# Attention by pairs of heads: two heads side by side in the TensorE array, values as the standing operand, probabilities scaled ahead of their transposes

## The chip, the cores and the metric

The kernel runs on one core of a Trainium2 chip, as one program written by hand for five engines: TensorE (PE in the profile, PEld for its weight loads), VectorE (DVE), ScalarE (ACT), GpSimd (POOL) and SyncE (SP), which issues the transfers. The metric is device time in microseconds (us), the median of several runs.

## The reference, cut to what matters

A block of two transformer layers and a second block of one layer, for 256 tokens of width 1024, all in float32. Each of the three layers has an attention, and these are what the change touches:

```python
# layer 0: 8 heads of 128 + 64 rotary; a query of chunk c (64 tokens) sees the keys of chunks <= c
s = (einsum('bqhd,bkhd->bhqk', qn, k_nope) + einsum('bqhr,bkr->bhqk', qr, k_rope)) * scale
p = softmax(where(key_chunk <= q_chunk, s, -inf));  o = einsum('bhqk,bkhd->bqhd', p, v);  y = o @ w_o
...
# layer 1: 16 heads of 64, a bias by relative position
p = softmax(where(valid, einsum('bnqhd,bnkhd->bnhqk', q, k_band) * 64**-0.5 + bias, -inf))
o = einsum('bnhqk,bnkhd->bnqhd', p, v_band) @ w_o
...
# second block: 8 heads of 64 by softmax with a bias, and 8 heads of 64 by stick-breaking
z = einsum('bhqd,bhkd->bhqk', qb, k) * scale
log_keep = where(past, log_sigmoid(-z), 0)
a = where(past, exp(log_sigmoid(z) + cumsum_from_the_right(log_keep) - log_keep), 0)
ob = einsum('bhqk,bhkd->bhqd', a, v)
```

With 256 tokens there are two blocks of 128 queries. Queries of the first block see only the first 128 keys, those of the second all 256, so the scores of a head are 128 x 128 and 128 x 256, stored as 128 partitions (queries) by 384 columns.

## The kernel before, in words

Activations stand transposed (features on partitions, 256 tokens along the columns). Every weight product is done in three float32r matmuls (high weight by high x, high by low, low by high: lines 448 to 450), and such a triple on one 128 x 128 weight tile is called a unit here. Weights come in pieces of 16 units (1 MB); ACT rounds a piece to its high half (L785, `whi`), DVE subtracts to get the low half (L1163, `wlo`), into three buffers each, so both run up to three pieces ahead of PE and wait for PE to finish a piece. Attention matmuls are plain float32, and each of these stands in the trace as two matmul records (two passes over the array).

An attention never stands alone on PE: the function `_mixed` deals its steps out between the units of the two weight products around it, and all engines walk the same list. Stage 0 is layer 0 (units of `wuq`, the query projection, then of `wo0`, the output projection), stage 1 is layer 1 (`wq1`, `wo1`), stage 2 the second block (`win_q`, then `win_g`, with eight softmax heads and then eight stick heads). For each head h:

- `scores` (L536, L538): PE multiplies queries by keys into a PSUM bank. Heads of 64 use 64 of the array's 128 rows; in stage 0 a full product is followed by two rotary parts on 32 rows. DVE adds the mask or bias and takes the row maximum (`biased`, L1217 and L1219), makes the exponent's offset (`least`, L1225), and ACT takes the exponential with its row sum (`exps`, L825 and L826).
- `turn` (L547): three transposes of the 128 x 384 probabilities; ACT copies them out of PSUM (`turned`, L834, tile `PT`).
- `values` (L557 to L559): the transposed probabilities are the standing operand and the head's values stream through, which gives queries on partitions; DVE scales by the inverse row sum while it copies to tile `O` (`output`, L1244).
- `chunk` (L567, L568): two transposes bring `O` (one head of 128 or two of 64) back to features on partitions; ACT makes the high half (`oh`, L839) and DVE the low half (`ol`, L1252) that the output projection reads.

Stick heads have `sticks` (L719, L720) for `scores`, then ACT, DVE and POOL work and `sums` (L725 to L727, sums of logarithms by a triangular matrix) before `values`. Four PSUM banks go round for the attention. An output projection's unit k*8 may not start before `chunk` k is done. The queries of a head must first be taken out of PSUM (`scaled_out`, L1261, on DVE), which stands in DVE's list at the last unit of their pair of tiles.

Of the kernel before, what the change touches and what calls it, by code (L numbers as in the profile page):

```python
# [7 lines left out]
F32 = mybir.dt.float32  # L8
# [84 lines left out]
def _soft_steps(heads, depth, per):  # L93

    ahead, whole = [], []
    for h in list(heads) + [None] * depth:
        before = ahead.pop(0) if len(ahead) == depth or (h is None and ahead) else None
        if before is not None:
            yield "turn", before
        if whole:  # L100
            yield "chunk", whole.pop(0)
        if h is not None:
            yield "scores", h
            ahead.append(h)
        if before is not None:
            yield "values", before
            if before % per == per - 1:
                whole.append(before // per)
    yield "chunk", whole.pop(0)


def _stick_steps(heads):
    ahead, whole = [], []
    for h in list(heads) + [None] * 2:
        before = ahead.pop(0) if len(ahead) == 2 or (h is None and ahead) else None
        if before is not None:
            yield "sums", before
        if whole:
            yield "chunk", whole.pop(0)
        if h is not None:  # L120
            yield "sticks", h
            ahead.append(h)
        if before is not None:
            yield "values", before
            if before % 2 == 1:
                whole.append(before // 2)
    yield "chunk", whole.pop(0)


def _mixed(units, steps, paces, head_at, chunk_name):  # L130
# [7 lines left out]

    for unit in units:
        if unit[0] == chunk_name:  # L140
            while unit[1] // 8 not in made:
                made.add(peek()[1] if peek()[0] == "chunk" else None)
                yield ahead.pop(0)
        yield unit
        done.add(unit)
        credit += paces[unit[0]]
        while credit >= 1:
            credit -= 1
            step = peek()
            if step is None or (step[0] in ("scores", "sticks") and head_at(step[1]) not in done):  # L150
                continue
            if step[0] == "chunk":
                made.add(step[1])
            yield ahead.pop(0)
# [1667 lines left out]
```

## Time and profile before

| | |
|---|---|
| three runs, median (lowest to highest) | 1096.03 us (1093.57 to 1100.73) |
| the profiled execution, its own time | 1088.3 us |
| its span, first to last instruction | 1086.6 us |
| mean granted TensorE clock | 0.974 |
| PE busy, PEld busy | 94%, 90% of the span |
| DVE busy, ACT busy | 67%, 50% |
| HBM read | 191.93 MB, 178 GB/s over the span |

Busy time of PE is made of modelled, overlapping records, so a matmul's cost is better read from the start of one record to the start of the next than from its length. The profile's span is 1.7 us below its execution's own time, and that is 0.7% below the median of the three runs.

### The profile page before, as it was taken

How to read it: one execution, taken by the hardware profiler on the slowest of the kernel's cores; microseconds unless marked ns; L12 is line 12 of the kernel's file. 1: busy time of each engine (PE TensorE's matmuls, PEld its weight loads, DVE VectorE, ACT ScalarE, POOL GpSimd, SP SyncE). 2: the span in 40 equal slices, each digit the busy share in tenths (PEclk: the TensorE clock that was granted, in tenths of full speed). 3: DMA queues.
4: the chain of work that ended last, by engine and by line, in shares of the span. 5: the costliest groups of instructions: out<-in, count | busy, mean ns of one | idle time of the engine just before them, and what ended most of it. 6: DMA issues, size and time to landing. Idle time of an engine off the chain costs nothing.

```text
span 1086.6 us, 19070 instructions
## 1 busy us (share of the span) xinstructions
PE 1022.5 (94%) x8068; PEld 976.2 (90%) x8068; DVE 729.1 (67%) x1300; ACT 538.4 (50%) x818; POOL 31.3 (3%) x50
## 2 busy tenths in 40 slices
PE   5989899999997999989999998899999989999997
PEld 5968799999996988879999996798999979999996
DVE  5845487787658855489786876545553776888762
ACT  6624464445434544455443432545664456666641
POOL 0000000000004000000000002000120000000000
PEclk9989999999998999999999998999999999999999
DMA  7512247666744723228665784352224344545541
GB/s 263 216 66 99 97 147 266 235 233 258 292 172 156 281 95 116 80 83 306 259 249 202 309 318 173 131 195 102 93 102 156 132 178 156 186 177 185 191 156 40
DMA packets 27877, 194.21 MB, mean 179 GB/s; under 512 B 3088, under 2 KB 3344, under 8 KB 4880
## 3 DMA queue, kind: packets, MB, share of 16 engines
q1 hardware_dynamic: 27792, 192.99, 48.5%
q8 instruction: 64, 1.05, 0.4%
q14 instruction: 21, 0.17, 0.0%
HBM read 191.93 MB, written 1.05 MB: 178 GB/s over the span
## 4 chain that ended last, share of the span: by engine, by line
PE 71%; DVE 13%; ACT 11%; issue 3%; DMA 1%; SPq 0%; POOL 0%; DVEq 0%; POOLq 0%; ACTq 0%
PE bank L448 19%; PE bank L450 18%; PE bank L449 18%; ACT s_whi L785 6%; DVE s_xT L1290 2%; PE bank L538 2%; DVE s_tmp L1613 2%; DVE s_tmp L1615 2%; PE bank L536 2%; PE bank L487 2%; DVE s_wlo L1163 2%; PE bank L489 1%; PE bank L488 1%; DVE s_tmp L1286 1%; ACT s_tmp L1123 1%
## 5 line engine op out<-in xcount | busy, mean ns | idle before, releaser
L1163 DVE TENSOR_TENSOR s_wlo<-s_raw,s_whi 128x512 fp32r<-128x512 f32 (+1 forms) x352 | 371.1, 1091 | 155.0 <-ACT s_whi L785 154.6
L448 PE MATMUL bank<-s_hh,s_whi 128*128 128x256 f32 x1560 | 447.3, 287 | 24.6 <-DVE s_wlo L1163 12.8
L449 PE MATMUL bank<-s_hl,s_whi 128*128 128x256 f32 x1560 | 438.4, 281 | 0.0
L450 PE MATMUL bank<-s_hh,s_wlo 128*128 128x256 f32 x1560 | 438.1, 281 | 0.0
L785 ACT ACTIVATE s_whi<-s_raw 128x1024 fp32r<-128x1024 f32 (+2 forms) x223 | 303.5, 1385 | 223.5 <-PE bank L450 209.2
L448 PEld LDWEIGHTS bank<-s_hh,s_whi 128*128 128x128 f32 x1560 | 298.9, 192 | 33.6 <-issue 15.4
L450 PEld LDWEIGHTS bank<-s_hh,s_wlo 128*128 128x128 f32 x1560 | 298.6, 191 | 0.0
L449 PEld LDWEIGHTS bank<-s_hl,s_whi 128*128 128x128 f32 x1560 | 298.2, 191 | 0.1
L448 PE MATMUL bank<-s_ph,s_whi 128*128 128x256 f32 x528 | 146.1, 277 | 0.5 <-DVE s_wlo L1163 0.5
L450 PE MATMUL bank<-s_ph,s_wlo 128*128 128x256 f32 x528 | 146.0, 277 | 0.0
L449 PE MATMUL bank<-s_pl,s_whi 128*128 128x256 f32 x528 | 146.0, 276 | 0.0
L448 PEld LDWEIGHTS bank<-s_ph,s_whi 128*128 128x128 f32 x528 | 99.1, 188 | 0.7 <-DVE s_wlo L1163 0.7
L450 PEld LDWEIGHTS bank<-s_ph,s_wlo 128*128 128x128 f32 x528 | 99.3, 188 | 0.0
L449 PEld LDWEIGHTS bank<-s_pl,s_whi 128*128 128x128 f32 x528 | 99.1, 188 | 0.0
L825 ACT ACTIVATE s_S<-s_S,s_small 128x128 f32<-128x128 f32 x32 | 12.8, 402 | 78.2 <-DVE s_small L1225 78.1
L1185 DVE SCALAR_TENSOR_TENSOR s_adacc<-s_raw,s_cact,s_adacc 128x2048 f32<-128x2048 f32 x21 | 49.2, 2344 | 0.0
L448 PE MATMUL bank<-s_oh,s_whi 128*128 128x256 f32 x128 | 38.0, 297 | 2.8 <-DVE s_Q L1261 1.7
L1406 DVE TENSOR_TENSOR s_tmp<-bank,s_R 128x256 f32<-128x256 f32 x44 | 18.5, 420 | 32.3 <-PE bank L450 32.3
L1613 DVE SCALAR_TENSOR_TENSOR s_tmp<-bank,s_cols,s_tmp 128x255 f32<-128x255 f32 (+1 forms) x44 | 21.2, 482 | 25.4 <-ACT s_tmp L1123 24.6
L487 PE MATMUL bank<-s_whi,s_hh 128*128 128x512 f32 x64 | 27.7, 433 | 8.6 <-DVE s_hl L1205 5.9
L449 PE MATMUL bank<-s_ol,s_whi 128*128 128x256 f32 x128 | 35.6, 278 | 0.0
L450 PE MATMUL bank<-s_oh,s_wlo 128*128 128x256 f32 x128 | 35.5, 278 | 0.0
(207 smaller groups left out, 1277.9 us busy)
## 6 DMA issues: line engine op xcount, KB each, us to landing
s_raw<-in_gu SPq DMA_DIRECT2D x44, 1024.0 KB, 4.9
s_raw<-in_dn SPq DMA_DIRECT2D x33, 1024.0 KB, 5.0
s_raw<-in_wada SPq DMA_DIRECT2D x24, 1024.0 KB, 5.4
s_raw<-in_up SPq DMA_DIRECT2D x22, 1024.0 KB, 4.9
s_raw<-in_wo SPq DMA_DIRECT2D x8, 1024.0 KB, 4.8
s_raw<-in_win_g SPq DMA_DIRECT2D x8, 1024.0 KB, 4.8
s_raw<-in_wkv_v SPq DMA_DIRECT2D x4, 1024.0 KB, 5.0
s_raw<-in_wkv_k SPq DMA_DIRECT2D x4, 1024.0 KB, 7.9
```

Of the source, the lines that this page charges most:

```text
L448: e.matmul(out, hi, xh[:, k, :], start=first, stop=False, skip_group_check=True)
L449: e.matmul(out, hi, xl[:, k, :], start=False, stop=False, skip_group_check=True)
L450: m = e.matmul(out, lo, xh[:, k, :], start=False, stop=last, skip_group_check=True)
L487: e.matmul(out, xh[:, k, xk], hi, start=k == 0, stop=False)
L536: e.matmul(bank[:, 0:P], x[:, 0:P], y[:, 0:P], start=i == 0, stop=i == n - 1)
L538: m = e.matmul(bank[:, P:384], x[:, P:T], y, start=i == 0, stop=i == n - 1)
L785: e.activation(whi[w % SPLIT][:, at], raw[p % RAW][:, at], ACT.Copy).then_inc(S.hi.tick((w, c0)), 1)
L1163: e.tensor_tensor(wlo[s][:, at], raw[p % RAW][:, at], whi[s][:, at].bitcast(F32), ALU.subtract).then_inc(S.lo.tick((i, j), (i, "all")), 1)
L1185: m = e.scalar_tensor_tensor(out=adacc[:, :], in0=src, scalar=cact[:, kc:kc + 1], in1=adacc[:, :], op0=ALU.mult, op1=ALU.add)
L1290: e.tensor_tensor(xT[:, j, :], xT[:, j, :], u[:, :], ALU.add).then_inc(S.resid.tick((nxt, j), (name, j)), 1)
L1613: e.scalar_tensor_tensor(out=v[:, shift:T], in0=bank[:, 0:T - shift], scalar=col(name, n), in1=v[:, shift:T], op0=ALU.mult, op1=ALU.add)
L1615: m = e.scalar_tensor_tensor(out=g[:, shift:T], in0=bank[:, T:2 * T - shift], scalar=col(name, NF + n), in1=g[:, shift:T], op0=ALU.mult, o ...
```

## The change: what it does

The step of the list is now a pair of heads, and the list has new steps (`scale`, `exp`). Five things differ:

- `scores` and `sticks` write two heads into two banks, with the matmuls of the two heads in turn. The heads of a pair lie on different rows of the array (rows 0 to 63 and 64 to 127; in stage 0 the rotary parts on neighbouring groups of 32 rows).
- `scale` (`normal`): DVE multiplies the probabilities by the inverse row sum in SBUF, before the transposes, in four instructions a pair.
- `values`: the head's values stand in the array and the transposed probabilities stream, so the result comes with features on partitions. Heads of 64 go to output partitions 0 to 63 and 64 to 127 of one bank (two halves of the array's columns). `output`, the tile `O` and the PE step `chunk` are gone; ACT and DVE make `oh` and `ol` straight from the bank, in stage 0 for two heads (512 columns) at once.
- the list deals pairs out by other paces; `scale`, `exp` and `chunk` take no place of their own on PE.
- the buffers: two `S` of two heads for three of one; the second `PT` of stages 0 and 1 lies in tiles `adacc` and `yb`; in stage 2 five banks go round; POOL's and ACT's stick work is done by pairs, two of ACT's three functions in one instruction for both heads.

```diff
+def _soft_steps(pairs):
+    pairs = list(pairs)
+    for i in range(-2, len(pairs)):
+        now, nxt, new = ((pairs[j:j + 1] if j >= 0 else []) for j in (i, i + 1, i + 2))
+        for p in new:
+            yield "scores", p
+        for p in now:
+            yield "values", p
+        for p in nxt:
+            yield "scale", p
+        for p in new:
+            yield "exp", p
+        for p in now:
+            yield "chunk", p
+        for p in nxt:
+            yield "turn", (p, 0)
+            yield "turn", (p, 1)
...
-    return _mixed(_units("wuq") + _units("wo0"), _soft_steps(range(8), 1, 1), {"wuq": 0.4, "wo0": 0.5},
-                  lambda h: ("wuq", 12 + 6 * (h // 2) + 5), "wo0")
+    return _mixed(_units("wuq") + _units("wo0"), _soft_steps(range(4)), {"wuq": 0.3, "wo0": 0.3},
+                  lambda p: ("wuq", 12 + 6 * p + 5), "wo0", 2)
...
-    return _mixed(_units("wq1") + _units("wo1"), _soft_steps(range(16), 2, 2), {"wq1": 0.6, "wo1": 0.6},
+    return _mixed(_units("wq1") + _units("wo1"), _soft_steps(range(8)), {"wq1": 0.35, "wo1": 0.35},
...
-                for i, (x, y) in enumerate(parts):
-                    e.matmul(bank[:, 0:P], x[:, 0:P], y[:, 0:P], start=i == 0, stop=i == n - 1)
-                for i, (x, y) in enumerate(parts):
-                    m = e.matmul(bank[:, P:384], x[:, P:T], y, start=i == 0, stop=i == n - 1)
...
+                for i, heads in enumerate(parts):
+                    last = i == len(parts) - 1
+                    for blk, cols_, rows in ((0, slice(0, P), P), (1, slice(P, 384), T)):
+                        for a, (x, y) in enumerate(heads):
+                            m = e.matmul(pair_banks[a][:, cols_], x[:, blk * P:(blk + 1) * P], y[:, 0:rows],
+                                         start=i == 0 and blk == 0, stop=last, skip_group_check=True)
...
-                e.matmul(bank[:, 0:dv], p[:, 0:P], A.V[:, 0, v], start=True, stop=True)
-                e.matmul(bank[:, dv:2 * dv], p[:, P:T], A.V[:, 0, v], start=True, stop=False)
-                e.matmul(bank[:, dv:2 * dv], p[:, T:384], A.V[:, 1, v], start=False, stop=True).then_inc(
-                    S.attn.tick((s, "values", h)), 1)
-            def chunk(s, A, c, per, b=None):
...
-                e.transpose(bank[:, 0:P], A.O[c % 2][:, 0, :], ident[:, :])
-                e.transpose(bank[:, P:T], A.O[c % 2][:, 1, :], ident[:, :]).then_inc(S.attn.tick((s, "chunk", c)), 1)
+                for kb, keys in ((0, slice(0, T)), (1, slice(T, 384))):
+                    for a in range(2):
+                        v = A.V[:, kb, (2 * p + a) * dv:(2 * p + a + 1) * dv]
+                        if dv == P:
+                            out, first = bank[:, a * T + kb * P:(a + 1) * T], a == 0 and kb == 0
+                        else:
+                            out, first = bank[a * dv:(a + 1) * dv, kb * P:T], kb == 0
+                        m = e.matmul(out, v, probs[:, a, keys], start=first, stop=kb == 1, skip_group_check=True)
+                m.then_inc(S.attn.tick((s, "values", p)), 1)
...
+            def normal(s, A, p):
+                w = small[p % 3]
+                q.wait_ge(S.soft, (s, "exp", p))
+                e.reciprocal(w[:, 12:16], w[:, 8:12]).then_inc(S.score.tick((s, p, "inverse")), 1)
+                q.wait_ge(S.score, (s, p, "inverse"))
+                for a in range(2):
+                    sc = A.S[p % 2][:, a, :]
+                    for blk, at in ((0, slice(0, P)), (1, slice(P, 384))):
+                        i = 2 * a + blk
+                        m = e.tensor_scalar(sc[:, at], sc[:, at], w[:, 12 + i:13 + i], None, ALU.mult)
+                    m.then_inc(S.score.tick((s, p, "scaled", a)), 1)
...
-                elif step == "values":
-                    output("o0", A0, i, P)
+                elif step == "scale":
+                    normal("o0", A0, i)
```

**PE in stage 1.** Before, where one head's scores and another's values stand (`qh`, `ql`: the layer's input; `bank`: PSUM):

```order
L536 MATMUL bank<-s_K,s_Q 128x128
L538 MATMUL bank<-s_K,s_Q 128x256
L448 MATMUL bank<-s_qh,s_whi 128x256
L449 MATMUL bank<-s_ql,s_whi 128x256
L450 MATMUL bank<-s_qh,s_wlo 128x256
L557 MATMUL bank<-s_V,s_PT 128x64
L558 MATMUL bank<-s_V,s_PT 128x64
L559 MATMUL bank<-s_V,s_PT 128x64
```

The same place after, for a pair's scores and the pair of values two pairs earlier:

```order
L541 MATMUL bank<-s_K,s_Q 128x128 x2
L541 MATMUL bank<-s_K,s_Q 128x256 x2
L448 MATMUL bank<-s_qh,s_whi 128x256
L449 MATMUL bank<-s_ql,s_whi 128x256
L450 MATMUL bank<-s_qh,s_wlo 128x256
L448 MATMUL bank<-s_qh,s_whi 128x256
L449 MATMUL bank<-s_ql,s_whi 128x256
L450 MATMUL bank<-s_qh,s_wlo 128x256
L569 MATMUL bank<-s_PT,s_V 64x256 x2
L569 MATMUL bank<-s_PT,s_V 64x128 x2
```

Two heads' scores now stand together, and values write 64 partitions with 256 and 128 streamed columns where three matmuls of 64 columns stood.

**ACT in stage 0, after the first scores.** Before, from the high half of a `wo0` piece to the next:

```order
L785 ACTIVATE s_whi<-s_raw 128x1024 [waits product_made,raw_in1]
L825 ACTIVATE s_S,s_small<-s_S,s_small 128x128 [waits biased_scores_made]
L826 ACTIVATE s_S,s_small<-s_S,s_small 128x256
L834 ACTIVATE s_PT<-bank 128x384 [waits attention_product_made]
L785 ACTIVATE s_whi<-s_raw 128x1024
```

After, between the same two weight instructions:

```order
L788 ACTIVATE s_whi<-s_raw 128x1024 [waits product_made,raw_in1]
L832 ACTIVATE s_S,s_small<-s_S,s_small 128x128 [waits biased_scores_made]
L832 ACTIVATE s_S,s_small<-s_S,s_small 128x256
L832 ACTIVATE s_S,s_small<-s_S,s_small 128x128
L832 ACTIVATE s_S,s_small<-s_S,s_small 128x256
L788 ACTIVATE s_whi<-s_raw 128x1024
```

The second weight instruction, which DVE's next low halves and then the second pair's queries stand behind, now comes after the exponentials of two heads.

**ACT in stage 0, at the first `wo0` unit.** Before:

```order
L785 ACTIVATE s_whi<-s_raw 128x1024 [waits product_made,raw_in2]
L825 ACTIVATE s_S,s_small<-s_S,s_small 128x128 [waits biased_scores_made]
L826 ACTIVATE s_S,s_small<-s_S,s_small 128x256
L785 ACTIVATE s_whi<-s_raw 128x1024
L785 ACTIVATE s_whi<-s_raw 128x1024 [waits product_made,raw_in3]
L834 ACTIVATE s_PT<-bank 128x384 [waits attention_product_made]
L839 ACTIVATE s_oh<-bank 128x256 [waits attention_product_made]
```

After:

```order
L788 ACTIVATE s_whi<-s_raw 128x1024 [waits product_made,raw_in2]
L832 ACTIVATE s_S,s_small<-s_S,s_small 128x128 [waits biased_scores_made]
L832 ACTIVATE s_S,s_small<-s_S,s_small 128x256
L832 ACTIVATE s_S,s_small<-s_S,s_small 128x128
L832 ACTIVATE s_S,s_small<-s_S,s_small 128x256
L846 ACTIVATE s_oh<-bank 128x512 [waits attention_product_made]
L788 ACTIVATE s_whi<-s_raw 128x1024
```

The copy of the first pair's output (`oh`), which the very first `wo0` unit needs, now stands behind the exponentials of the third pair; before, the first chunk stood well ahead of this place (the `oh` row shown is the second).

## Rows read from the trace of the kernel before

**Rows 1.** The page: the chain that ended last, shares of the span by engine.

```profile
PE 71%; DVE 13%; ACT 11%; issue 3%; DMA 1%; SPq 0%; POOL 0%; DVEq 0%; POOLq 0%; ACTq 0%
```

**Rows 2.** Windows of stages 0, 1, 2: length, busy time by engine, clock, DMA.

```profile
61.77:130.34 68.57, 65.49 (x430) 55.99 (x431) 32.26 (x97) 27.29 (x61) 0.00 (x0) 0.93 0.22 79
385.41:465.46 80.05, 75.05 (x560) 66.68 (x561) 44.80 (x166) 41.20 (x104) 0.00 (x0) 1.00 0.26 90
733.71:820.51 86.80, 84.61 (x627) 76.90 (x627) 47.99 (x143) 49.52 (x109) 10.65 (x32) 1.00 0.30 104
```

**Rows 3.** Who waited for whom on PE in stage 1: total us, times, longest.

```profile
PE bank L536 <- DVE s_Q L1261: 2.1, 2, 1.2
PE bank L567 <- DVE s_O L1244: 1.6, 2, 1.4
```

**Rows 4.** Timeline of PE, stage 1, a head's scores and values: start, us, instruction.

```profile
389.38 0.28 PE L450 MATMUL bank<-s_qh,s_wlo 128*128 128x256 f32 x1
389.59 0.48 PE L536 MATMUL bank<-s_K,s_Q 64*128 64x128 f32 x2
...
390.66 0.28 PE L449 MATMUL bank<-s_ql,s_whi 128*128 128x256 f32 x1
390.78 0.29 PE L450 MATMUL bank<-s_qh,s_wlo 128*128 128x256 f32 x1
...
391.70 0.28 PE L449 MATMUL bank<-s_ql,s_whi 128*128 128x256 f32 x1
```

**Rows 5.** Timeline of PE, stage 0: scores, values and chunk of one head.

```profile
94.68 0.28 PE L450 MATMUL bank<-s_oh,s_wlo 128*128 128x256 f32 x1
...
97.66 0.29 PE L449 MATMUL bank<-s_ol,s_whi 128*128 128x256 f32 x1
...
98.12 0.28 PE L450 MATMUL bank<-s_oh,s_wlo 128*128 128x256 f32 x1
...
99.03 0.28 PE L449 MATMUL bank<-s_ol,s_whi 128*128 128x256 f32 x1
...
100.43 0.28 PE L449 MATMUL bank<-s_ol,s_whi 128*128 128x256 f32 x1
100.54 0.28 PE L450 MATMUL bank<-s_oh,s_wlo 128*128 128x256 f32 x1
...
101.00 0.28 PE L449 MATMUL bank<-s_ol,s_whi 128*128 128x256 f32 x1
```

**Rows 6.** Timeline of PE, stage 2: the sums of a stick head.

```profile
781.89 0.59 PE L725 MATMUL bank<-s_PT,s_tri 128*128 128x256 f32 x2
782.32 0.38 PE L726 MATMUL bank<-s_PT,s_negones 128*128 128x128 f32 x2
782.54 0.39 PE L727 MATMUL bank<-s_PT,s_tri 128*128 128x128 f32 x2
```

**Rows 7.** Timeline of PE, stage 0: the first scores, with the wait before them.

```profile
61.77 1.94 PE L536 MATMUL bank<-s_K,s_Q 128*128 128x128 f32 x6 [4.47 <-DVE s_Q L1261]
```

**Rows 8.** Timeline of DVE: bias, offset and low half after scores.

```profile
66.91 0.29 DVE L1217 CUSTOM_DVE_ANT_0 s_S<-bank,s_mask 128x128 f32<-128x128 f32 x1 [5.19 <-PE bank L538]
...
67.58 0.17 DVE L1225 TENSOR_SCALAR s_small<-s_small 128x2 f32<-128x2 f32 x1
...
71.30 0.69 DVE L1163 TENSOR_TENSOR s_wlo<-s_raw,s_whi 128x512 fp32r<-128x512 f32 x1 [2.32 <-ACT s_whi L785]
```

**Rows 9.** Timeline of ACT: exponentials of one head, the next high half.

```profile
67.79 0.40 ACT L825 ACTIVATE s_S<-s_S,s_small 128x128 f32<-128x128 f32 x1 [10.01 <-DVE s_small L1225]
...
68.59 0.19 ACT L826 ACTIVATION_READ_ACCUMULATOR s_S<-s_S,s_small 128x1 f32 x1
...
70.22 1.05 ACT L785 ACTIVATE s_whi<-s_raw 128x1024 fp32r<-128x1024 f32 x1
```

**Rows 10.** DVE by form: eviction of queries, a multiply in SBUF; count, busy us, mean ns.

```profile
L1261 DVE TENSOR_TENSOR s_Q<-bank,s_R 128x256 f32<-128x256 f32 x20 | 7.5, 417 | 5.9 <-PE bank L450 3.6 <-ACT s_R L816 2.4
...
L1314 DVE TENSOR_SCALAR s_tmp<-s_tmp 128x256 f32<-128x256 f32 x1 | 0.3, 296 | 0.0
```

More of the change, by code:

```diff
@@ L90, in _used_up, with _stick_steps, _mixed @@
     return FIRST[name] + (-(-t // PIECE) if t == COUNT[name] else t // PIECE)
[L93 to L130, printed above, removed]
+def _soft_steps(pairs):
[15 more added lines that the diff above has]
+            yield "turn", (p, 1)
+def _stick_steps(pairs):
+    pairs = list(pairs)
+    for i in range(-2, len(pairs)):
+        now, nxt, new = ((pairs[j:j + 1] if j >= 0 else []) for j in (i, i + 1, i + 2))
+        for p in now:
+            yield "values", p
+        for p in new:
+            yield "sticks", p
+        for p in now:
+            yield "chunk", p
+        for p in nxt:
+            yield "sums", p
+def _mixed(units, steps, paces, pair_at, chunk_name, per=1):
     steps, ahead, done, made, credit = iter(steps), [], set(), set(), 0.0
@@ L137, in peek, with taken @@
         return ahead[0] if ahead else None
+    def taken():
+        step = ahead.pop(0)
+        if step[0] == "chunk":
+            made.update(range(step[1] * per, (step[1] + 1) * per))
+        return step
     for unit in units:
@@ L141, in _mixed @@
             while unit[1] // 8 not in made:
-                made.add(peek()[1] if peek()[0] == "chunk" else None)
-                yield ahead.pop(0)
+                peek()
+                yield taken()
         yield unit
@@ L146, in _mixed @@
         credit += paces[unit[0]]
[L147 to L154, printed above, removed]
+        while peek() is not None and (credit >= 1 or ahead[0][0] in ("scale", "exp", "chunk")):
+            if ahead[0][0] in ("scores", "sticks") and pair_at(ahead[0][1]) not in done:
+                credit = min(credit, 1.0)
+                break
+            if ahead[0][0] not in ("scale", "exp", "chunk"):
+                credit -= 1
+            yield taken()
     while peek() is not None:
-        yield ahead.pop(0)
+        yield taken()
 def _units(name):
@@ new lines, in tensor_program @@
+                    q.wait_ge(S.act_out, ("win_k", i // 2 * 2))
+                    q.wait_ge(S.act_out, ("win_q", i // 2 * 2))
+                    (heads,) = half_parts(A2, i)
+                    pair_banks = []
+                    for a in range(2):
+                        b = 3 + 2 * (i % 2) + a
+                        pair_banks.append(take(b, S.dve_tmp, ("least", i, a)))
+                        bank_of["sticks", i, a] = b
+                    for a, (x, y) in enumerate(heads):
+                        e.matmul(pair_banks[a][:, 0:T], y[:, 0:P], x, start=True, stop=True, skip_group_check=True)
@@ L1255, in scaled_out, with chunk @@
+            def chunk(s, A, p, n):
+                bank = banks[bank_of[s, "values", p]]
+                q.wait_ge(S.xhi, (s, p))
+                to = slice(n * p, n * (p + 1))
+                src = pair(bank) if n == 2 else bank[:, 0:T].rearrange("p (a b) -> p a b", a=1)
+                e.tensor_tensor(A.ol[:, to, :], src, A.oh[:, to, :].bitcast(F32), ALU.subtract).then_inc(
+                    S.xlo.tick((s, p), *((s, "o", c) for c in range(n * p, n * (p + 1)))), 1)
             def scaled_out(name, n, m, R, s, to):
```

350 lines of the change are left out of this document (160 added, 190 removed).

## The prediction

> **What bounds the kernel now.** I read the chain that ended last first: PE has 71% of it [rows 1], so what shortens PE's own list shortens the time. Then I cut out the three stretches in which attention is dealt out between weight units, from the first score to the end of that stage's last chunk or sum, and looked at how much of each PE is not busy [rows 2]: 68.57 - 65.49 = 3.1 us in stage 0, 5.0 in stage 1, 2.2 in stage 2. DVE and ACT are busy about half of each, and DMA a quarter: PE is the bound there, and a nanosecond less on PE is a nanosecond less in time until a wait takes its place. Of the 5.0 us in stage 1, 2.1 are waits of scores for queries that DVE takes out of PSUM (one of them ends just as the stage begins), and 1.6 waits of the chunk's transposes for the output scaling [rows 3]; the second kind has no successor after the change.
>
> **What a block costs on PE.** I take a block's price as the time from the start of the last unit matmul before it to the start of the second one behind it, less two unit matmuls of 0.115 us (100.43 to 100.54 in [rows 5]); so what a block does to its neighbours is in it. In us:
> - scores of a head in stage 0: 97.66 - 94.68 - 0.23 = 2.75; values 99.03 - 98.12 - 0.23 = 0.68; chunk 101.00 - 100.54 - 0.23 = 0.23 [rows 5].
> - scores of a head in stage 1: 390.66 - 389.38 - 0.23 = 1.05; values 391.70 - 390.78 - 0.23 = 0.69 [rows 4]. Stage 2 has the same shapes, sticks too.
>
> A float32 matmul is two passes. On the full array a pass of 256 columns takes (782.32 - 781.89) / 2 = 0.215 and one of 128 columns (782.54 - 782.32) / 2 = 0.11 [rows 6]. Six full-array passes of values are then 0.66 of the 0.68 paid, so full-array float32 costs nothing extra. Scores of stage 1 use 64 rows (the form 64*128 in [rows 4]): passes 2 x 0.11 + 2 x 0.215 = 0.65, paid 1.05, so a trip into a part-array form and back costs 0.40. Scores of stage 0 make two such trips (full, 32 rows, full, 32 rows): 3 x 0.65 = 1.95, and 2.75 - 1.95 = 0.80, twice 0.40. The Trainium skill says in TensorEngine Tiling (Array Packing), Key Properties, that changing the tiling mode, not just the tile, drains the engine; the 0.40 fits that, and the same list says that tiles of one mode run in parallel, which no run here shows yet.
>
> **The change on PE.** The trace has no two heads in the array at once, so I bound it from both sides. Serial: every pass waits for the last one. Staggered: instructions start in order, the two passes of one matmul follow each other, but the second pass of one head runs beside the first pass of the other. That is what the program permits (other rows or other columns, other banks or partitions), so I take staggered and keep serial for the range.
> - Scores of a pair in stage 0: one trip instead of four. Full passes 1.30, rotary passes 2.60 serial or 0.11 + 0.11 + 0.215 x 3 + 0.11 + 0.215 x 3 = 1.62 staggered, plus 0.40: 4.30 or 3.32, against 5.50.
> - Values of a pair in stage 0: full array, 4 x 0.215 + 4 x 0.11 = 1.30 against 1.36; two chunks, 0.46, go.
> - Scores of a pair in stages 1 and 2: 1.30 + 0.40 = 1.70 serial; staggered 0.11 + 0.11 + 3 x 0.215 + 0.40 = 1.27; against 2.10.
> - Values there: twice the streamed passes and a new trip into half-column form (price unseen; nearest row, the 64-row trip): 1.70 serial, 1.27 staggered, against 1.38. One chunk, 0.23, goes. Values alone gain little or lose.
>
> Stage 0, 4 pairs: 4 x (1.20 + 0.52) = 6.9 serial, 4 x (2.18 + 0.52) = 10.8 staggered. The 8 + 4 + 4 pairs of stages 1 and 2: 16 x (0.40 - 0.32 + 0.23) = 5.0 serial, 16 x (0.83 + 0.11 + 0.23) = 18.7 staggered. **PE gains 11.9 to 29.5 us.** By the Trainium skill (TensorE: Matmul & The Clock Gate, Measured speedup vs the span model) four row tiles ran 3.07 times as fast, 0.77 of four; by that, the part-array passes, serial 4 x 2.60 + 32 x 1.30 = 52 us, would take 52 / (2 x 0.77) = 34, an estimate that is also what the staggered passes add up to, so it would leave the forecast where it is; no run here shows it.
>
> **Waits that come and go.** Work off PE stays about equal: per pair, the output's four DVE scalings become four in SBUF (256 columns take 0.30 there, [rows 10]), ACT does the same exponentials. What changes is who stands behind whom, since two heads are now handled at once. After a pair's scores DVE needs two heads x 0.67 (67.58 - 66.91) and 0.17 for the offset [rows 8], ACT two heads x 0.99 (67.79 to 68.78) for the exponentials [rows 9].
> - Stage 0, second scores. They follow directly on the last unit of their queries. DVE's eviction of those (2 x 0.42, [rows 10]) stands behind low halves of 0.69 that wait for a high half of 1.05 on ACT [rows 8, 9], which now stands behind four exponentials: 0.1 + 1.5 + 2.0 + 1.05 + two low halves 1.3 + 0.8 = 6.7 after the first scores, while PE has six units, some 4 us since it is then at the lower of its two clock levels, 1.2 GHz: after an idle 4.47 six score records take 1.94 [rows 7], where six passes of 0.11 and a trip make 1.1. About 2.8 of wait.
> - First transposes: they wait for bias, offset, inverse and two scalings, 1.5 + 0.2 + 0.5 + hops 0.2 = 2.4, with three units (1.0) as cover: 1.3, once in each stage.
> - First `wo0` unit: needs the first chunk, whose copy on ACT stands behind the third pair's exponentials and whose low half on DVE behind scalings, two low halves and an eviction: bias 1.5, low halves 1.3, eviction 0.8, scalings 1.2, low half of 512 columns 0.7 = 5.4 after the scores, and PE has 1.0 + 1.3 of work: 3.1. The next chunk is late by some 0.3. An idle stretch like this may also bring the clock down for a while as [rows 7] shows after 4.47: 1.0 for that.
> - Stage 0 then idles 2.8 + 1.3 + 3.1 + 0.3 and the closing 0.9 = 8.4 against 3.1. Stage 1: first transposes 1.3, third scores behind their eviction 1.4, first `wo1` unit behind the last eviction 1.1, closing 0.9: 4.7 against 5.0. Stage 2: 1.2, third scores behind ACT's eviction 1.0, and in the stick part sums and values with five units (1.7) as cover for a chain of about 2.0 through DVE, ACT and POOL, four times 0.3 and once for the sums: 3.7 against 2.2.
>
> Waits cost 5.3 - 0.3 + 1.5 + 1.0 = 7.5. Edits at no cost: the moved `PT` (its new wait, on the last values of stage 0, stands before adaptive-norm work that comes a stage later), POOL's selections (as many as before), transfers (none is moved; weights are up to three pieces ahead). A pair's chunk makes DVE wait for ACT's copy, and weight low halves stand behind that; those three pieces cover it, and where they are used up it costs PE the same 1 us or so per pair as in the second rival below. In the steady part the transposes are covered: scalings end about 2.8 to 3.2 after the scores, PE comes to them after five or six units and the values, 3.0 to 3.3. The cover is thin.
>
> **Sum.** 29.5 - 7.5 = 22 us off the profiled execution: 1088.3 - 22 = 1066. The median of the runs lies 0.7% above that execution, so I give 1096 - 21 = 1075 as a median.
>
> **Rivals.**
> - Serial: the halves don't overlap in float32. 11.9 - 7.5 = 4 less, 1092. For it: nothing in the trace shows two at once. Against: unit matmuls start 0.11 apart with records of 0.28 [rows 5], so what follows a matmul inside one form is hidden already.
> - The cover of the steady part fails. One more low half and an eviction on DVE ahead of a pair's scaling (0.69 + 0.8 - 0.2 of margin = 1.3) in each of the 13 softmax pairs after the first of a stage: 17 late, 1075 + 17 = 1092. For it: DVE is the engine that now does scaling between exponentials and transposes. Against: half of DVE is free [rows 2].
> - Slower: each change from one head to the other costs half a trip, 0.20, as a change of form does. There are 7 changes in stage 0's scores, 3 in other scores, 3 in values: 4 x 7 + 16 x 6 = 124, 24.8 on top of serial: 1092 + 25 = 1117. It decides from 0.1 per change. For it: all changes of rows in the trace cost this much. Against: these were also changes of size, and here only the place changes.
>
> **How the numbers follow.** Staggered as summed 0.70 (gains of 11 to 32), serial 0.14, cover fails 0.09, slower 0.07. About 1%, 11 us, is what a measurement of this kernel tells from no change. Faster by more: 0.66 of the first and 0.02 of the second and third, 0.68; within: 0.24; slower: the last and a little of serial, 0.08. The range leaves out the slower rival, serial's upper half and gains over 32: 1064 to 1094.
>
> **What would show it.** Right: in stages 1 and 2 scores and values of a pair each near 1.3 by the same measure, in stage 0 scores near 3.3, no transposes from `O`, and PE's idle time concentrated at each stage's start and at the first `wo0` unit. Wrong: matmuls of the two heads a full pass apart (serial), longer than a pass apart (slower), or waits of each pair's transposes for DVE's scaling. A lower clock in other places, or weights that arrive late because PE asks sooner, would also break the sum.

## The result, and the profile after

The changed kernel takes 1086.24 us, median of 20 runs (1075.63 to 1097.72), beside 1095.47 for the kernel before, also of 20 (1085.31 to 1104.08). The ratio is 0.9905, 95% interval 0.9876 to 0.9934: 9 to 10 us, 0.95%, faster. The forecast was 1075, range 1064 to 1094: the sign and the range hold, the gain is about half of the 21 us forecast. The execution that was profiled after the change ran 1% slower than the median (own time 1097.72, clock 0.954) also in code that the change doesn't touch, so spans of stages are compared here and not whole executions.

The chain of waits, which was 71% PE [rows 1], on the page of the changed kernel:

```profile
PE 79%; DVE 10%; ACT 8%; issue 2%; DMA 1%; POOL 0%; SPq 0%; DVEq 0%; POOLq 0%; ACTq 0%
```

Windows of the three stages of the changed kernel, from the first score to the end of the last attention block, as in [rows 2]: window and length, busy time of PE, PEld, DVE, ACT, POOL with counts, the granted clock, DMA share, GB/s.

```profile
61.04:126.98 65.94, 60.03 (x398) 53.87 (x399) 29.76 (x85) 26.28 (x57) 0.00 (x0) 0.81 0.24 83
388.17:460.08 71.91, 63.49 (x512) 55.13 (x513) 43.51 (x150) 39.78 (x104) 0.00 (x0) 0.98 0.28 100
734.10:821.50 87.40, 73.17 (x542) 65.18 (x542) 42.55 (x115) 45.88 (x100) 11.24 (x32) 0.90 0.26 92
```

Against 68.57, 80.05 and 86.80 before, stage 0 is 2.6 us shorter, stage 1 8.1, and stage 2 0.6 longer. The windows of stages 0 and 1 hold the same weight units before and after (82 and 112), but that of stage 2 holds 114 where it held some 127. From the first to the last unit matmul of stage 2, PE alone, before and then after:

```profile
727.27:837.50 110.23, 107.21 (x826) 1.00 0.32 115
727.65:842.70 115.05, 99.98 (x778) 0.93 0.31 110
```

With equal work around it stage 2 is 4.8 us longer. PE is busy 5.5 us less in stage 0, 11.6 in stage 1 and 7.2 in stage 2, part of it at the lower clock, so its work fell by more than that. But it now idles 65.94 - 60.03 = 5.9, 8.4 and 14.2 us in the three windows, and its clock there is 0.81, 0.98 and 0.90, where it was 0.93, 1.00 and 1.00.

**PE's blocks.** Timeline of PE in stage 1 of the changed kernel, the scores of a pair (x8) and the values of a pair (x8) between weight units, for [rows 4]:

```profile
410.13 0.28 PE L450 MATMUL bank<-s_qh,s_wlo 128*128 128x256 f32 x1
410.33 0.93 PE L541 MATMUL bank<-s_K,s_Q 64*128 64x128 f32 x8
411.19 0.39 PE L448 MATMUL bank<-s_qh,s_whi 128*128 128x256 f32 x1
411.41 0.28 PE L449 MATMUL bank<-s_ql,s_whi 128*128 128x256 f32 x1
...
412.22 0.28 PE L450 MATMUL bank<-s_qh,s_wlo 128*128 128x256 f32 x1
412.42 0.87 PE L569 MATMUL bank<-s_yb,s_V 128*64 128x256 f32 x8
413.22 0.39 PE L448 MATMUL bank<-s_qh,s_whi 128*128 128x256 f32 x1
413.44 0.28 PE L449 MATMUL bank<-s_ql,s_whi 128*128 128x256 f32 x1
```

By the prediction's measure the scores of a pair cost 411.41 - 410.13 - 0.23 = 1.05. One head cost 1.05 before [rows 4]: the second head is free. Values of a pair cost 413.44 - 412.22 - 0.23 = 0.99, where two heads cost 1.38. The same timeline cut to 0.06 us shows two records that have begun, the first passes of both heads:

```profile
410.33 0.38 PE L541 MATMUL bank<-s_K,s_Q 64*128 64x128 f32 x2
```

Timeline of PE in stage 0 of the changed kernel, the scores of a pair, for [rows 5]:

```profile
84.58 0.28 PE L450 MATMUL bank<-s_cqh,s_wlo 128*128 128x256 f32 x1
84.70 2.98 PE L541 MATMUL bank<-s_K,s_Q 128*128 128x128 f32 x24
87.61 0.38 PE L448 MATMUL bank<-s_cqh,s_whi 128*128 128x256 f32 x1
87.83 0.28 PE L449 MATMUL bank<-s_cql,s_whi 128*128 128x256 f32 x1
```

87.83 - 84.58 - 0.23 = 3.02 for a pair, where two heads cost 5.50.

**PE's waits.** Who waited for whom on PE in the changed kernel (total us, times, longest), in stage 1, for [rows 3]:

```profile
PE bank L552 <- DVE s_S L1251: 5.0, 3, 4.2
PE bank L541 <- DVE s_Q L1268: 1.7, 2, 0.9
```

and in stage 2:

```profile
PE bank L569 <- POOL s_S L1678: 8.7, 4, 3.2
PE bank L552 <- DVE s_S L1251: 3.8, 1, 3.8
```

L552 are the transposes, L569 the values. In stages 1 and 2 nearly all the waiting for scaled probabilities is one wait of some 4 us, at the first transposes. In the stick part PE waits for POOL's selection at every pair's values, three times about 3 us.

The first transposes of stage 1: timelines of ACT, DVE and PE of the changed kernel in one window, the lines that follow each other in the chain.

```profile
390.64 0.40 ACT L832 ACTIVATE s_S<-s_S,s_small 128x128 f32<-128x128 f32 x1 [6.70 <-DVE s_small L1239]
...
392.41 1.04 ACT L788 ACTIVATE s_whi<-s_raw 128x1024 fp32r<-128x1024 f32 x1
393.48 0.69 DVE L1175 TENSOR_TENSOR s_wlo<-s_raw,s_whi 128x512 fp32r<-128x512 f32 x1 [2.88 <-ACT s_whi L788]
394.09 0.28 DVE L1230 CUSTOM_DVE_ANT_0 s_S<-bank,s_bias 128x128 f32<-128x128 f32 x1
...
395.60 1.01 DVE L1251 TENSOR_SCALAR s_S<-s_S,s_small 128x128 f32<-128x128 f32 x4
...
396.30 0.62 PE L552 MATMUL bank<-s_ident,s_S 128*128 128x128 f32 x3 [4.21 <-DVE s_S L1251]
```

ACT is idle for 6.70 us and then does the first pair's four exponentials; the weight's high half stands behind them in its list and starts at 392.41. DVE's next entry is the low half of that weight: it waits 2.88 for it. Behind the low half stand the second pair's bias (394.09), and only then the first pair's scaling (395.60), though its exponentials were done at 392.4. Nothing here is slow: the first pair's scaling stands in DVE's list behind work that it doesn't need, and that work waits for ACT.

The stick part of the changed kernel, first pair: DVE, ACT, POOL and PE between the sums (the last one starts at 781.46 on PE) and the values.

```profile
781.36 1.03 DVE L1543 SCALAR_TENSOR_TENSOR s_PT<-s_S,s_PT 128x384 f32<-128x384 f32 x2 [1.13 <-ACT s_S L1080]
782.31 1.47 DVE L1175 TENSOR_TENSOR s_wlo<-s_raw,s_whi 128x512 fp32r<-128x512 f32 x2
783.70 1.01 DVE L1549 TENSOR_SCALAR s_S<-bank 128x384 f32<-128x384 f32 x2
```

```profile
784.27 0.99 ACT L1085 ACTIVATE s_S<-s_S 128x384 f32<-128x384 f32 x2 [1.05 <-DVE s_S L1549]
```

```profile
784.86 0.59 POOL L1676 TENSOR_SCALAR_AFFINE_SELECT s_S<-s_S 128x128 f32<-128x128 f32 x1 [0.69 <-ACT s_S L1085]
...
786.35 0.29 POOL L1678 TENSOR_SCALAR_AFFINE_SELECT s_S<-s_S 128x128 f32<-128x128 f32 x1
```

```profile
786.79 1.55 PE L569 MATMUL bank<-s_S,s_V 128*64 128x256 f32 x8 [3.22 <-POOL s_S L1678]
```

From the sums to the values 5 us pass. On DVE a step of the second pair's sticks (L1543, 1.0) and two low halves (1.4) stand ahead of the first pair's entry at 783.70, and POOL's selections for the pair take 1.8 (784.86 to 786.64). PE has five units, 1.7 us, to cover all that.

**PE's clock.** Windows of PE alone in the changed kernel behind such waits (length, busy, clock, DMA share, GB/s):

```profile
61.04:82.56 21.52, 19.18 (x81) 0.50 0.14 49
396.50:400.10 3.60, 3.60 (x20) 0.53 0.02 5
742.14:748.15 6.01, 6.01 (x28) 0.50 0.29 70
785.70:792.50 6.80, 5.71 (x27) 0.50 0.42 154
802.80:806.20 3.40, 3.40 (x19) 0.50 0.79 251
```

0.50 is 1.2 GHz instead of 2.4. The first stretch follows the 4.76 us wait for the rotary part of the queries, which the kernel before has too [rows 7]; it lasts on past the second scores, which wait 2.72. The third follows the first transposes of stage 2, the others the waits shown above.

### The profile page after: what moved, and what is told of

Its sections match the earlier page's. It is cut to its first block, busy times and chain, and to the rows that moved or that the text cites. A ratio compares the mean times of both kernels' runs of the same rounds, so it can differ in the third digit from the quotient of the medians.

```text
span 1095.3 us, 18728 instructions
## 1 busy us (share of the span) xinstructions
PE 1011.3 (92%) x7940; PEld 968.4 (88%) x7940; DVE 722.8 (66%) x1248; ACT 533.2 (49%) x806; POOL 31.8 (3%) x50
## 3 DMA queue, kind: packets, MB, share of 16 engines
q8 instruction: 62, 1.02, 0.3%
HBM read 191.93 MB, written 1.05 MB: 176 GB/s over the span
## 4 chain that ended last, share of the span: by engine, by line
PE 79%; DVE 10%; ACT 8%; issue 2%; DMA 1%; POOL 0%; SPq 0%; DVEq 0%; POOLq 0%; ACTq 0%
PE bank L448 23%; PE bank L449 22%; PE bank L450 22%; ACT s_whi L788 2%; PE bank L541 2%; DVE s_xT L1297 2%; DVE s_wlo L1175 2%; PE bank L487 2%; PE bank L489 1%; PE bank L488 1%; PE bank L569 1%; PE bank L552 1%; DVE s_tmp L1293 1%; ACT s_S L832 1%; PE bank L510 1%
## 5 line engine op out<-in xcount | busy, mean ns | idle before, releaser
L448 PE MATMUL bank<-s_hh,s_whi 128*128 128x256 f32 x1560 | 449.1, 288 | 27.1 <-DVE s_wlo L1175 14.2
L449 PE MATMUL bank<-s_hl,s_whi 128*128 128x256 f32 x1560 | 442.9, 284 | 0.0
L450 PE MATMUL bank<-s_hh,s_wlo 128*128 128x256 f32 x1560 | 442.8, 284 | 0.0
L448 PEld LDWEIGHTS bank<-s_hh,s_whi 128*128 128x128 f32 x1560 | 304.3, 195 | 35.6 <-issue 17.4
L449 PE MATMUL bank<-s_pl,s_whi 128*128 128x256 f32 x528 | 148.4, 281 | 0.0
L450 PE MATMUL bank<-s_ph,s_wlo 128*128 128x256 f32 x528 | 148.4, 281 | 0.0
L448 PE MATMUL bank<-s_ph,s_whi 128*128 128x256 f32 x528 | 148.4, 281 | 0.0
L832 ACT ACTIVATE s_S<-s_S,s_small 128x128 f32<-128x128 f32 x64 | 28.3, 445 | 59.1 <-DVE s_small L1239 59.1
L541 PE MATMUL bank<-s_K,s_Q 64*128 64x128 f32 (+5 forms) x192 | 28.7, 394 | 10.1 <-DVE s_Q L1268 8.5
```

The source lines that it names most:

```text
L448: e.matmul(out, hi, xh[:, k, :], start=first, stop=False, skip_group_check=True)
L449: e.matmul(out, hi, xl[:, k, :], start=False, stop=False, skip_group_check=True)
L450: m = e.matmul(out, lo, xh[:, k, :], start=False, stop=last, skip_group_check=True)
L541: m = e.matmul(pair_banks[a][:, cols_], x[:, blk * P:(blk + 1) * P], y[:, 0:rows], start=i == 0 and blk == 0, stop=last, skip_group_check= ...
L832: m = e.activation(sc[:, at], sc[:, at], ACT.Exp, scale=scale, bias=w[:, 4 + i:5 + i], accum_out=w[:, 8 + i:9 + i])
```

## The experiments

A number of a stage is, in this section, the time from the start of the stage's first weight-unit matmul to the start of its last one in the profile. Units have the same order and number in all kernels, so it can be compared everywhere. The changed kernel has 20 runs, e2, e3 and e8 ten each, the others four.

| kernel | stage 0 | stage 1 | stage 2 | sum | median us | ratio to before, 95% |
|---|---|---|---|---|---|---|
| before | 79.01 | 85.33 | 110.23 | 274.57 | 1095.47 | |
| after | 76.45 | 77.19 | 115.04 | 268.68 | 1086.24 | 0.9905 [0.9876, 0.9934] |
| e1_exp_late | 71.96 | 73.04 | 110.05 | 255.05 | 1074.5 | 0.9798 [0.9719, 0.9877] |
| e2_stick_cover | 71.89 | 78.83 | 114.41 | 265.13 | 1081.82 | 0.9895 [0.9851, 0.9938] |
| e3_unpaired | 83.68 | 77.42 | 112.93 | 274.03 | 1093.15 | 0.9986 [0.9947, 1.0025] |
| e4_late_cover | 68.80 | 73.00 | 108.54 | 250.34 | 1064.11 | 0.9725 [0.9651, 0.9800] |
| e5_chunk_first | 71.40 | 73.01 | 98.61 | 243.02 | 1059.52 | 0.9685 [0.9645, 0.9725] |
| e6_filler | 69.63 | 75.53 | 107.74 | 252.90 | 1071.11 | 0.9778 [0.9730, 0.9827] |
| e7_first_and_filler | 67.27 | 73.01 | 98.29 | 238.57 | 1055.35 | 0.9650 [0.9595, 0.9705] |
| e8_before_filler | 80.92 | 86.86 | 110.20 | 277.98 | 1087.39 | 0.9954 [0.9908, 0.9999] |

Each ratio is to runs of the kernel before on the same chip, whose median was 1093.1 to 1095.6.

Stage 0 has the same code in `after` and in e2_stick_cover, and still differs by 4.6 us: how long PE stays at the lower clock there differs between executions (the granted clock from 48 to 126 us is 0.82 in `after` and 0.96 in e2_stick_cover).

My theory was that PE's part of the change works, and that the missing half of the gain lies in waits that come from the order of ACT's, DVE's and POOL's lists, and in the clock behind them. The rivals: that the pairing itself gives less than it seems, or that DVE (with ACT and POOL) has too much to do, which no order would mend.

### e1_exp_late

In the dealing-out of steps, the first pair's exponentials are held back, by three units in stage 0 and by one in the others (`left`), so that ACT's next high half stands ahead of them. Nothing moves on PE.

```diff
...
             if ahead[0][0] in ("scores", "sticks") and pair_at(ahead[0][1]) not in done:
                 credit = min(credit, 1.0)
                 break
+            if ahead[0] == ("exp", 0) and left > 0:
+                left -= 1
+                break
...
```

> The first pair's exponentials are issued one weight unit later in stages 1 and 2 and three units later in stage 0, so that ACT's next high half stands ahead of them; nothing on TensorE moves. Theory (the waits at the start of each stage come from one queue: high half behind four exponentials, low half behind the high half, bias, scaling or query eviction behind the low half): the first transposes wait 1.0 to 1.5 us in stages 1 and 2 instead of 4.5 and 4.1, the second scores of stage 0 wait 0.5 instead of 2.7, and with shorter waits the clock is not lowered behind them; 2.2 + 3.3 + 2.9 of waits and about 8 of half clock, 12 to 18 us less than the changed kernel. Rival (DVE simply has too much to do for two heads before the first transposes): the waits stay within 0.5 us and the time within 3 us. If only the waits matter and the clock falls all the same: 6 to 9 us less.

Measured: 1074.5, 11.7 us below the changed kernel. Waits of PE in stage 1:

```profile
PE bank L555 <- DVE s_S L1254: 2.2, 3, 1.4
```

where it was 5.0 with a longest of 4.2; in stage 2 the first transposes start 1.24 us after the matmul ahead of them (4.08 before this edit), in stage 0 the second scores 1.26 (2.72) and the first transposes 1.27 (0.45). Stage 1 becomes 4.2 us shorter, stage 2 5.0. There is no half clock behind the first transposes any more. So the queue is the cause and DVE's load isn't: it does the same work. In stage 0 the edit proves nothing: the stage is as short in e2_stick_cover, which lacks it. The gain is a little below the 12 expected at least.

### e2_stick_cover

In the stick part, the next pair's sums come ahead of the sticks of the pair after it.

```diff
         for p in now:
             yield "values", p
+        for p in nxt[:1 if i >= 0 else 0]:
+            yield "sums", p
         for p in new:
             yield "sticks", p
         for p in now:
             yield "chunk", p
-        for p in nxt:
+        for p in nxt[:1 if i < 0 else 0]:
             yield "sums", p
```

> In the stick part the sums of the next pair now come before the scores of the one after it, so that ten weight units and a block stand between the sums and the values of a pair instead of five units; the pace stays. Theory (the 3 us waits of the stick values are a latency chain through DVE, ACT and POOL with too little cover): three of the four waits (3.5, 3.1, 2.8) fall below 0.5 us, the first pair's stays at about 3.5 since its place is the same, no half clock behind the later ones: 6 to 10 us less than the changed kernel. Rival (DVE, ACT and POOL together can't keep the pace of stick pairs): the wait moves to the sums, which then have five units less ahead of them, and the time stays within 2 us.

Measured: 1081.82, ratio 0.9895, not to be told from the changed kernel. The values now follow 3.50, 2.62 and 2.63 us behind the matmul ahead of them (3.50, 3.06, 2.77 in the changed kernel): neither theory. The waits stay at the values and don't go to the sums, which speaks against the rival; but they now end on DVE, by the waits of PE in stage 2:

```profile
PE bank L571 <- DVE s_ol L1261: 4.9, 3, 2.4
```

e4_late_cover shows what that is. The first transposes of stages 1 and 2, which this edit doesn't touch, wait as in the changed kernel: 4.49 and 4.07 from start to start (4.49 and 4.08 there).

### e3_unpaired

Inside a block, all matmuls of one head come before those of the other (scores, sticks and values alike).

```diff
-                for i, heads in enumerate(parts):
-                    last = i == len(parts) - 1
-                    for blk, cols_, rows in ((0, slice(0, P), P), (1, slice(P, 384), T)):
-                        for a, (x, y) in enumerate(heads):
+                for a in range(2):
+                    for i, blk, cols_, rows in [(i, *k) for i in range(len(parts))
+                                                for k in ((0, slice(0, P), P), (1, slice(P, 384), T))]:
+                        last = i == len(parts) - 1
+                        for x, y in parts[i][a:a + 1]:
...
```

> The same work, orders and layouts, but inside each scores, sticks and values block all matmuls of one head come before those of the other, so nothing is left to run side by side except where one head's last pass meets the other's first. Theory (what the change gains is that the two heads' passes run at the same time): a pair's scores cost 1.7 to 1.9 instead of 1.0 in stages 1 and 2 and about 4.5 instead of 2.9 in stage 0, values 1.5 to 1.7 instead of 1.0; 20 to 28 us more on TensorE, of which a little falls into waits that are there anyway: 15 to 25 us slower than the changed kernel, slower than the kernel before. Rival (the gain comes from fewer changes of form and from the chunk transposes that fell away): within 5 us of the changed kernel.

Measured: 1093.15, 6.9 us slower than the changed kernel; I had expected 15 to 25. That is neither theory nor rival. In stages 1 and 2 the blocks cost what they did: scores 1.06, values 1.01. The order of the list made no difference there. The timeline of PE cut to 412.7 to 412.8, where the list now has four passes of the first head ahead of the second head's first one, shows two records begun:

```profile
412.74 0.39 PE L542 MATMUL bank<-s_K,s_Q 64*128 64x128 f32 x2
```

The two heads' matmuls run as two streams; the second head's doesn't wait for the first head's to be done. All the loss is in stage 0, where a full-array matmul stands between the rotary parts of the two heads:

```profile
88.88 0.28 PE L450 MATMUL bank<-s_cqh,s_wlo 128*128 128x256 f32 x1
89.00 4.67 PE L542 MATMUL bank<-s_K,s_Q 128*128 128x128 f32 x24
93.60 0.38 PE L448 MATMUL bank<-s_cqh,s_whi 128*128 128x256 f32 x1
93.82 0.28 PE L449 MATMUL bank<-s_cql,s_whi 128*128 128x256 f32 x1
```

93.82 - 88.88 - 0.23 = 4.71, the serial 1.30 + 2.60 and two trips of 0.40 together; 4 x (4.71 - 3.02) = 6.8, about the whole difference (7.2 in stage 0, 6.9 in the medians). So running side by side is worth what it seems, and my idea of how it comes about was wrong.

### e4_late_cover

The edits of e1_exp_late and e2_stick_cover together.

> Both moves together: late first exponentials and the new order of the stick steps. Theory: the two gains add, since they lie in different places: 18 to 28 us less than the changed kernel, about 1060, 30 or so below the kernel before. Rival (an engine other than TensorE carries the stages): less than the larger of the two alone plus 3 us.

Measured: 1064.11, 22.1 us below the changed kernel, within what was expected. Waits of PE in stage 2:

```profile
PE bank L574 <- DVE s_ol L1264: 4.9, 3, 2.4
PE bank L574 <- POOL s_S L1683: 3.2, 1, 3.2
```

Only the first pair's values still wait for POOL. The later ones wait for DVE to empty their bank, the chunk of the pair before. On DVE's timeline it is the last of these three:

```profile
763.39 1.01 DVE L1543 TENSOR_SCALAR s_PT<-bank 128x384 f32<-128x384 f32 x2
764.91 1.03 DVE L1548 SCALAR_TENSOR_TENSOR s_PT<-s_S,s_PT 128x384 f32<-128x384 f32 x2 [0.51 <-ACT s_S L1085]
765.85 0.42 DVE L1264 TENSOR_TENSOR s_ol<-bank,s_oh 128x256 fp32r<-128x256 f32 x1
```

It stands behind two steps of the next sticks, which wait for three passes of ACT.

### e5_chunk_first

On top of e4_late_cover, the chunk comes right behind the next sums, and a step that does nothing (five units) stands ahead of the first stick values. The diff is against the changed kernel, without the lines of e1_exp_late.

```diff
+        for p in now[:1 if i == 0 else 0]:
+            yield "rest", p
         for p in now:
             yield "values", p
         for p in nxt[:1 if i >= 0 else 0]:
             yield "sums", p
-        for p in new:
-            yield "sticks", p
         for p in now:
             yield "chunk", p
+        for p in new:
+            yield "sticks", p
...
```

> The kernel with late first exponentials and sums ahead of the next sticks, and two moves more in the stick part: a pair's chunk steps stand right behind the next pair's sums, no longer behind the next sticks on DVE, and five weight units more stand ahead of the first stick values. Theory (in the version before this one the stick values no longer wait for POOL but for their bank, which DVE frees only behind the offsets of the next sticks; the first ones for POOL with five units of cover): waits of 3.5, 2.6 and 2.6 us fall below 0.6 each, no half clock in the stick part: 7 to 11 us less than that version, 1053 to 1057. Rival (DVE, ACT and POOL can't do a stick pair in the time that TensorE takes for fifteen units and the blocks): the waits move to the sums or sticks and the time stays within 3 us.

Measured: 1059.52, 4.6 us below e4_late_cover where 7 to 11 were expected, with intervals that overlap; in the profiles stage 2 is 9.9 us shorter, as expected, and has no half clock. Waits in stage 2:

```profile
PE bank L576 <- POOL s_S L1685: 1.5, 1, 1.5
PE bank L576 <- DVE s_ol L1266: 0.5, 1, 0.5
```

Of 8.1 us of waits 2.0 are left, 1.5 of them ahead of the first pair's values, where less than 0.6 was expected. The rival falls: DVE, ACT and POOL keep the pace.

### e6_filler

The changed kernel with its order and its waits, and useless matmuls ahead of eight of them, as here ahead of the first transposes.

```diff
...
+                for _ in range({('o1', 0, 0): 18, ('o2', 0, 0): 16}.get((s, p, a), 0)):
+                    e.matmul(bank[:, 0:P], ident[:, :], ident[:, :], start=True, stop=True, skip_group_check=True)
                 q.wait_ge(S.score, (s, p, "scaled", a))
...
```

> The changed kernel with the waits as they are, but ahead of eight of them TensorE does useless 128-column matmuls on the identity into a bank that is overwritten afterwards, sized a little below the wait seen (18 ahead of stage 0's first scores, 11 ahead of its second scores and of its first output unit, 18 and 16 ahead of the first transposes of stages 1 and 2, 13, 11 and 10 ahead of three stick values). No engine but TensorE does anything else. If half clock behind the waits is a loss of its own: the stretches at half clock go and about 8 to 15 us with them. If the chains on DVE, ACT and POOL set the ends of these waits and half clock mostly hides in the next wait: 0 to 6 us. If the filler delays what follows: slower by up to 5 us.

Measured: 1071.11, 15.1 us below the changed kernel. Windows of PE over the same places:

```profile
48.11:82.70 34.59, 31.45 (x257) 1.00 0.25 92
380.20:395.00 14.80, 12.98 (x111) 1.00 0.25 84
760.00:790.00 30.00, 29.54 (x248) 1.00 0.22 75
```

The clock is 1.00 where it was 0.50, and no list but PE's has changed: the transposes of stage 1 still come 4.4 us after the unit ahead of them. So the clock behind the waits was a loss of its own, nearly as large as the waits. Part of it isn't due to the change: behind its first scores the kernel before runs at the lower clock too (0.93 over stage 0, [rows 2]).

### e7_first_and_filler

The order of e5_chunk_first, and filler ahead of the first scores and the first output unit of stage 0.

> The version with all moves of the order, and useless matmuls in two waits that remain: 18 ahead of stage 0's first scores (4.8 us of wait for the rotary part of the queries, there in the kernel before too) and 11 ahead of its first output unit (3.0 us). If half clock behind these waits is a loss: stage 0 does its first scores and the units behind them in half the time, 3 to 6 us less than the same version without filler. If the chain through DVE and ACT sets the next wait anyway: within 2 us.

Measured: 1055.35, 4.2 below e5_chunk_first, in the expected range but with intervals that overlap. In the profile stage 0 is 4.1 us shorter and the other stages are the same. It has the lowest median: 3.5% below the kernel before.

### e8_before_filler

The kernel before, with the 18 useless matmuls ahead of its first scores.

> The kernel before, with 18 useless 128-column matmuls ahead of its first scores of stage 0, where TensorE waits 4.75 us for the rotary part of the queries and then runs at half clock for some 10 us. If what the filler gave the last version has nothing to do with the change, the same place gives it here: 3 to 5 us less than the kernel before. If the kernel before loses nothing there because its next scores wait for their queries anyway: within 1 us.

Measured: 1087.39, ratio 0.9954 [0.9908, 0.9999], 5.7 us below the kernel before (1093.13 in the runs beside it). But in its profile stage 0 is longer (80.92 against 79.01) and the clock 0.68 between 60.0 and 66.9 us and 0.50 from there to 76.0: the filler didn't hold it there. The granted clocks of the ten runs go with their times: seven runs had 0.976 to 0.983 over the whole program and took 1081.51 to 1089.83 us, the other three, the profiled one among them, 0.958 to 0.971 and 1093.85 to 1100.84; the 13 runs of the kernel before beside them had 0.966 to 0.976. So the filler seems to raise the clock in most executions, which agrees with the first case, and the profile is of one in which it didn't; a profile of the others isn't there to show it.

## Why the prediction came out as it did

**PE's term was right in kind and too small.** Forecast 29.5 us, with serial passes as the other end. Counted again with the measured prices:

| block | count | before | forecast | after | gain |
|---|---|---|---|---|---|
| scores of a pair, stage 0 | 4 | 5.50 | 3.32 | 3.02 | 9.9 |
| values of a pair, stage 0 | 4 | 1.36 | 1.30 | 1.31 | 0.2 |
| scores or sticks of a pair, stages 1 and 2 | 16 | 2.10 | 1.27 | 1.05 | 16.8 |
| values of a pair, stages 1 and 2 | 16 | 1.38 | 1.27 | 0.99 | 6.2 |
| chunk transposes | 24 | 0.23 | 0 | 0 | 5.5 |

38.6 us, 9 more than the end I called best. The step that failed is "instructions start in order, the two passes of one matmul follow each other, but the second pass of one head runs beside the first pass of the other": the heads don't take turns pass by pass, both stream at once, and a pair's passes take as long as one head's. The Trainium skill says in TensorEngine Tiling (Array Packing), Key Properties, that tiles operate independently; the trace agrees, for scores in full: 1.05 for two heads as for one. The trip of 0.40 holds too: 1.05 is 2 x 0.11 + 2 x 0.215 and 0.40; into the half-column form of the values it is 0.99 - 0.65 = 0.34. The 34 us that the prediction worked out for all part-array passes was too long as well: by these prices they take half of the serial 52. The rivals "serial" and "slower" are refuted by these prices.

**The waits were too small in two places.** As forecast: stage 0's second scores 2.72 from start to start (2.8), its first output unit 2.96 (3.1), its first transposes 0.45 in this profile and 1.30 in e2_stick_cover's (1.3), the third scores of stages 1 and 2 1.12 and 1.02 (1.4, 1.0), the first `wo1` unit 1.13 (1.1). Wrong: the first transposes of stages 1 and 2, 4.49 and 4.08 against 1.3 and 1.2, and the stick values, 3.50, 3.06, 2.77 and 0.46 against 0.3 each. For the transposes the sum had bias, offset, inverse and scaling, but not the low half that stands among them in DVE's list and waits for a high half that waits for the pair's own exponentials. I had followed exactly this queue for stage 0's second scores, and not for the transposes. For the sticks it took a chain of 2.0 with nothing ahead of it on DVE; with a step of the next pair and two low halves ahead on DVE, and 1.8 of selections on POOL, it is 5. Idle time in the three windows came to 28.6 us, 18.3 more than before, where 6.5 more was forecast. (Two sums of the prediction are also 0.1 short: 2.4 - 1.0 is 1.4 for the first transposes, and the terms of the first `wo0` unit make 5.5.)

**The clock was too small by an order.** 1.0 was set aside. e6_filler, which changes only that, gives 15.1 us in the medians and 268.68 - 252.90 = 15.8 in the stages, 11.2 if stage 0 of the changed kernel is taken as e2_stick_cover ran it. Some 4 of these, by e7_first_and_filler against e5_chunk_first, lie in stage 0, where the kernel before loses clock as well.

So 38.6 less 18.3 less some 11 to 15 leaves 5 to 9; the medians gave 9 to 10, the stages of the two profiles 274.57 - 268.68 = 5.9. It is a rough account: the last two terms aren't independent, since a part of the half clock lies inside the next wait (stage 0's second scores wait 2.72 in the profile after and 4.41 in e2_stick_cover's, which came to them at full clock), and the clock term holds what the kernel before loses too. That the time fell into the range is luck in part: one term too small by 9 and two too small by 22 to 26 together.

**The rival "cover of the steady part fails"** did not come: behind the first transposes of stage 1, all others together wait 0.8 us.

**Order and clock are the missing half.** The mended order with the clock held (e7_first_and_filler) takes 36.0 us less in the three stages than the kernel before (274.57 - 238.57), beside PE's 38.6. Not all of that is the change's own: some 4 of it come from filler in stage 0, which would help the kernel before too. e5_chunk_first, without filler, takes 274.57 - 243.02 = 31.6 less.

## What to carry to other kernels

When work is handled in larger lumps, follow for the first lump of a stage every list that it goes through, with what stands ahead in it and what that waits for; a background task (here the next weight's high half) that could run in idle time loses its place as soon as the lump's work is listed ahead of it. Here a wait on the engine that bounds the kernel cost its length and, behind most of the long ones, several us at half clock, so gains on that engine had to be counted net of both. Useless matmuls in the waits, sized a little below them, were worth about as much as shortening the waits: 15.1 us in e6_filler, 11.7 in e1_exp_late.

## What was not expected of the hardware

Two heads in different rows (or columns) of the array ran as two independent streams: the price of a block was the same with the heads' matmuls alternating (scores 1.05, values 0.99) and one head after the other (1.06 and 1.01). A full-array matmul between them ended that: 4.71 instead of 3.02.

Waits of PE of 4.49, 4.08, 3.50 and 3.06 us in stages 1 and 2 were followed by about 3.4, 6.0, 5.7 and 3.4 us at half clock, one of 2.77 by none, and the 4.76 in stage 0 by 21.5 us that held a second wait; with filler in the waits the same places ran at 1.00. The length of a wait alone doesn't decide: the third stick values waited 2.76 in e1_exp_late and 2.63 in e2_stick_cover, and the clock over the next 4 us was 0.61 and 0.59, while behind the second ones of e2_stick_cover, which waited 2.62, it stayed 1.00. In the profiled execution of the kernel before with filler, the same filler at the same place of stage 0 left the clock at 0.68 and then 0.50, and it stays open why.
